# A two-block layer on one core: half of the query weights kept in place of two gather slots, expert products in quadrants

## The reference, cut to what matters

```python
beta = jax.nn.sigmoid(b.astype(f32))
g = -jnp.exp(A_log.astype(f32)) * jax.nn.softplus(a.astype(f32) + dt_bias.astype(f32))
```

```python
mod = (c_act @ w_ada[l] + b_ada[l])[:, None, :]
h = rms_norm(x, g_mix[l]) * (1.0 + scale1) + shift1
proj = h @ w_in[l]
q_a, lat, k_r, iq, ik, iw, q_b, k_b, v_b, f_b = jnp.split(proj, split_at, axis=-1)
o_a = dsa_attention(...)          # over keys that an index picks
o_b = forgetting_attention(...)   # f_b: 8 columns, one forget logit per head
mixed = jnp.concatenate([rms_norm(o_a, g_out_a[l]), rms_norm(o_b, g_out_b[l])], axis=-1)
x = x + gate1 * (mixed @ w_out[l])
h2 = rms_norm(x, g_ffn[l]) * (1.0 + scale2) + shift2
x = x + gate2 * peer_ffn(h2, w_peer_q[l], peer_keys1[l], peer_keys2[l], peer_u[l], peer_v[l])
```

```python
act = jax.nn.gelu(jnp.einsum('cd,chkd->chk', hc, u[expert]), approximate=False)
wgt = (g * act).astype(hc.dtype)
return jnp.einsum('chk,chkd->cd', wgt, v[expert])
```

## Time and profile before

| | us |
|---|---|
| three timed runs | 1416.09, 1419.27, 1419.91 |
| their median | 1419.27 |
| the profiled execution | 1415.75 |
| its span in the trace | 1413.8 |
| TensorE busy | 1301.3 (92%) |
| VectorE, ScalarE, GpSimd busy | 833.5, 275.1, 429.4 |
| DMA | 431.46 MB, mean 305 GB/s |
| granted TensorE clock, mean | 0.989 |

### The profile page before, as it was taken

The page is one execution under the profiler, slowest core; times in us unless marked ns, Lnnn a source line. Parts: engine busy times, 40 slices in busy tenths (PEclk is TensorE's granted clock), DMA queues, the critical chain, the costliest instruction groups (busy, mean ns, idle before and its releaser), DMA issues.

```text
span 1413.8 us, 15154 instructions
## 1 busy us (share of the span) xinstructions
PE 1301.3 (92%) x5447; PEld 837.9 (59%) x5447; DVE 833.5 (59%) x2027; ACT 275.1 (19%) x671; POOL 429.4 (30%) x554
## 2 busy tenths in 40 slices
PE   7999999999999999999999989889998777778776
PEld 6888888888687777757576634445642222222222
DVE  3553466203138888733476777757667667766654
ACT  2013100130010000033332235432220112111101
POOL 0101030000100000000034545555566555655551
PEclk9999999999999999999999999999999999999999
DMA  8345665224469888477369999999999999999995
GB/s 291 121 160 190 228 141 179 75 106 150 134 238 327 289 314 290 178 269 281 141 266 424 422 424 421 421 396 408 425 426 425 425 426 425 426 425 426 425 426 242
DMA packets 120250, 431.46 MB, mean 305 GB/s; under 512 B 10998, under 2 KB 35004, under 8 KB 84592
## 3 DMA queue, kind: packets, MB, share of 16 engines
q0 software_dynamic: 37904, 275.99, 47.6%
q1 hardware_dynamic: 82272, 154.50, 30.4%
HBM read 429.23 MB, written 1.24 MB: 304 GB/s over the span
## 4 chain that ended last, share of the span: by engine, by line
PE 57%; DMA 30%; ACT 4%; DVE 3%; issue 2%; POOL 2%; SPq 1%; POOLq 0%; DVEq 0%; ACTq 0%
PE psum L592 30%; DMA wr<-peer_uv,arena 18%; DMA arena<-peer_uv,arena 7%; PE psum L1140 6%; PE psum L906 4%; PE psum L882 2%; DMA xc<-peer_uv,arena 2%; DMA first_slot<-peer_uv,arena 2%; PE psum L1158 1%; PE psum L957 1%; DVE wr L2419 1%; PE psum L992 1%; POOL arena L2594 1%; PE psum L657 1%; PE psum L1202 1%
## 5 line engine op out<-in xcount | busy, mean ns | idle before, releaser
L592 PE MATMUL psum<-hT,wr 128*128 128x256 f32 x1728 | 377.5, 380 | 0.0
L592 PEld LDWEIGHTS psum<-hT,wr 128*128 128x128 f32 x1728 | 327.0, 190 | 48.1 <-issue 4.0
L1140 PE MATMUL psum<-wr,arena 128*128 128x512 f32 x576 | 277.5, 612 | 38.6 <-POOL arena L2594 38.5
L2419 DVE CUSTOM_DVE_ANT_0 wr<-psum,wr 128x1024 f32<-128x1024 f32 x144 | 176.0, 1222 | 105.7 <-DMA wr<-peer_uv,arena 105.4
L1140 PEld LDWEIGHTS psum<-wr,arena 128*128 128x128 f32 x576 | 102.3, 192 | 179.5 <-issue 178.4
L2594 POOL TENSOR_SCALAR arena<-cst,arena 128x128 f32<-128x128 f32 x256 | 122.7, 479 | 200.9 <-ACT arena L1569 189.4
L2622 POOL DMA_INDIRECT wr<-peer_uv,arena x144 | 143.8, 999 | 64.8 <-PE psum L1140 39.1
L1140 PE MATMUL psum<-arena 128*128 128x512 f32 x256 | 126.6, 619 | 32.7 <-POOL arena L2594 32.7
L1569 ACT ACTIVATE arena<-arena 128x1 f32<-128x1 f32 x256 | 50.8, 202 | 492.6 <-DVE arena L2419 492.2
L2419 DVE CUSTOM_DVE_ANT_0 arena<-psum,arena 128x1024 f32<-128x1024 f32 x64 | 78.3, 1224 | 55.4 <-DMA arena<-peer_uv,arena 55.4
L1140 PEld LDWEIGHTS psum<-arena 128*128 128x128 f32 x256 | 44.5, 192 | 109.9 <-issue 109.7
(11 more groups left out here) (354 smaller groups left out, 1449.4 us busy)
## 6 DMA issues: line engine op xcount, KB each, us to landing
wr<-in_w_in SPq DMA_DIRECT2D x21, 2048.0 KB, 9.0
arena<-in_w_ada SPq DMA_DIRECT2D x12, 2048.0 KB, 10.3
wr<-in_w_up SPq DMA_DIRECT2D x22, 1024.0 KB, 8.1
arena<-piece SPq DMA_DIRECT2D x16, 1024.0 KB, 9.3
wr<-in_w_down SPq DMA_DIRECT2D x5, 2048.0 KB, 9.6
wr<-in_w_a_out SPq DMA_DIRECT2D x2, 2048.0 KB, 8.0
wr<-in_w_b_out SPq DMA_DIRECT2D x2, 2048.0 KB, 8.0
wr<-in_w_o SPq DMA_DIRECT2D x2, 2048.0 KB, 8.1
```

What stands on the lines that cost most here:

```text
L592: mm = nc.tensor.matmul(bank[p % 4][:, f * S:(f + 1) * S], slot(i)[:, k, n * P:(n + 1) * P], act[:, k, :], start=k == 0, stop=k == KT - 1)
L1140: mm = nc.tensor.matmul(bank[(6, 0)[t] + half][:, :], diag[:, n % DIAGS, :], gring[slot_of][:, D + half * BANK:D + (half + 1) * BANK], sta ...
L2419: V.tensor_tensor_reduce(gring[slot_of][:, 0:D], h2[t], gring[slot_of][:, 0:D], 1.0, 0.0, ALU.mult, ALU.add, dots[:, t, c:c + 1]).then_inc ...
```

## The change

It does the following.

- The second half of the query weights stays in its `wr` buffer until tile 1 has used it; its two pieces are no longer read. The two slots that lay there join at set 118. The ring has 5 slots, 6 from the sixth set on, 9 from set 88, 13 from set 118 (before 7, 8, 11, 13). The diagonals are laid one ahead of the gather, not two.
- The expert product of a set is made in quadrants: four products of 64x64 diagonal blocks with 512 columns, in the order low/low, high/high, low/high, high/low (rows of the array, then output partitions), so that bank i holds the positions of half i and its partitions the column halves. `add_experts` puts them together with twice the products on 64 partitions.
- The gates' product is made as two sums of four terms for a and b each, in four groups of 8 output partitions (0, 32, 64, 96); VectorE adds the two sums.
- The forget weights are columns 440 to 447 of tok; `forget(t)` then is a transpose of those columns of `tokp`. The names fb0 and fb1 move later in TensorE's order, and their steps on VectorE and ScalarE with them.
- For tile 1, ScalarE makes `branch_stats(1, 1)` after the last attention step, not in step 6; it empties mb1 at tick 78, not 79, ahead of `branch_stats(1, 0)`; VectorE makes `branch_norm(1, 1)` at tick 76 and `branch_norm(1, 0)` at 81 (before 80). TensorE waits for `orow_done` ahead of the output projection.

```diff
-SLOTS, DIAGS, LAG, LEAD = 7, 8, 2, 2
+SLOTS, DIAGS, LAG, LEAD = 5, 8, 2, 1
...
+TOK = 440 + H
...
-JOIN = {SLOTS: 1, 88: 3, 118: 2}
+JOIN = {SLOTS: 1, 88: 3, 118: 4}
...
-    until("tok", w2[:, :, 512:952], 440, "pair_ready", PAIR["tok0"][0] + 1)
+    until("tok", w2[:, :, 512:952], TOK, "pair_ready", PAIR["tok0"][0] + 1)
...
+PIECES = len(PIECE_FROM) - 2
...
-        gring = [wr[(wpq0 + i // 2 - 1) % NS][:, (i % 2) * 2 * D:(i % 2 + 1) * 2 * D] for i in range(SLOTS - 1)]
-        gring = [first_slot[:, :]] + gring
-        gring += [xc[:, 0:2 * D]] + [region(kb0, 2 * D) for kb0 in (8, 19, 70, 50, 58)]
+        halves_of = [wr[(wpq0 + i // 2 - 1) % NS][:, (i % 2) * 2 * D:(i % 2 + 1) * 2 * D] for i in range(2 * NS)]
+        gring = [first_slot[:, :]] + halves_of[:SLOTS - 1] + [xc[:, 0:2 * D]]
+        gring += [region(kb0, 2 * D) for kb0 in (8, 19, 70, 50, 58)] + halves_of[SLOTS - 1:]
...
-            for k in range(KT):
-                mm = nc.tensor.matmul(bank[4][0:32 + H, 0:S], ab[:, k, :], hT[:, k, :], start=k == 0, stop=k == KT - 1)
+            for k in range(KT // 2):
+                for g in range(2):
+                    for half in range(2):
+                        o = 64 * g + 32 * half
+                        mm = nc.tensor.matmul(bank[4][o:o + H, 0:S], ab[:, half * KT // 2 + k, 32 * g:32 * g + H], hT[:, half * KT // 2 + k, :],
+                                              start=k == 0, stop=k == KT // 2 - 1)
...
+                emptied(pe, ("tok0", "tok1b")[t])
                 o = claim_bank(f"fb{t}")
-                pe.wait_ge(s["small_in"], 48)
-                for k in range(KT):
-                    mm = nc.tensor.matmul(o[0:H, 0:P], fbw[:, k, :], hT[:, k, tiles_of[t]], start=k == 0, stop=k == KT - 1)
-                mm.then_inc(s["pair_ready"], 1)
+                nc.tensor.matmul(o[0:H, 0:P], tokp[:, 440:TOK], ident, start=True, stop=True).then_inc(s["pair_ready"], 1)
...
-                if t == 0:
+                if t == 0 or j >= 2:
                     weights(at["wpq"] + j // 2)
                     w = slot(at["wpq"] + j // 2)[:, :, (j % 2) * 2 * P:(j % 2 + 1) * 2 * P]
...
-                    for half in range(2):
-                        mm = nc.tensor.matmul(bank[(6, 0)[t] + half][:, :], diag[:, n % DIAGS, :],
-                                              gring[slot_of][:, D + half * BANK:D + (half + 1) * BANK], start=c == 0, stop=c == P - 1)
-                        if n == SETS - 1 and half == 0:
-                            mm.then_inc(s["half_done"], 1)
+                    for i, cols in ((0, 0), (1, 1), (0, 1), (1, 0)):
+                        own = quarters[i]
+                        mm = nc.tensor.matmul(bank[(6, 0)[t] + i][quarters[cols], :], diag[own, n % DIAGS, own],
+                                              gring[slot_of][own, D + cols * BANK:D + (cols + 1) * BANK], start=c == 0, stop=c == P - 1)
                     mm.then_inc(s["pe_used"], 1)
...
                 if q == 0:
+                    pe.wait_ge(s["orow_done"], 2)
                     emptied(pe, "mb1")
...
             latent_stats(0)
+            copy_q(0, 0)
             forget(0)
-            copy_q(0, 0)
             copy_index(0)
...
-                if step == 6:
-                    branch_stats(1, 1)
-            until(att_tick(UNITS + 1) + 3)
+            branch_stats(1, 1)
+            until(T_TURN + 1)
+            turn_evac("mb1", 1, lambda k: vcol("g_out_b_2", k))
+            until(T_TURN + 2)
             branch_stats(1, 0)
-            until(T_TURN + 2)
-            turn_evac("mb1", 1, lambda k: vcol("g_out_b_2", k))
...
+            chain(V.tensor_copy(small[:, 5, :], bank[4][64:64 + H, 0:S]))
+            chain.wait()
+            chain(V.tensor_tensor(small[:, 0, :], small[:, 0, :], bank[4][32:32 + H, 0:S], ALU.add))
+            chain(V.tensor_tensor(small[:, 5, :], small[:, 5, :], bank[4][96:96 + H, 0:S], ALU.add))
...
+            def add_experts(t, first):
+
+                for n in range(2):
+                    c = slice(n * BANK, (n + 1) * BANK)
+                    for i, own in enumerate(quarters):
+                        chain(V.tensor_tensor(gated[own, n, :], bank[first + i][quarters[n], :], modb[quarters[n], 3, c], ALU.mult))
+                    chain.wait()
+                    V.tensor_tensor(x[:, t, c], x[:, t, c], gated[:, n, :], ALU.add).then_inc(s["x_final"], 1)
...
-            until(att_tick(UNITS - 1) + 3)
+            until(att_tick(UNITS) + 6)
             branch_norm(1, 1)
             until(att_tick(UNITS + 1) + 2)
             branch_rows(1, 0)
-            until(att_tick(UNITS + 1) + 5)
+            until(T_TURN + 4)
             branch_norm(1, 0)
-            until(T_TURN + 2)
             gain_evac(1)
...
-            dve.wait_ge(s["half_done"], 1)
-            for n in range(2):
-                c = slice(n * BANK, (n + 1) * BANK)
-                if n:
-                    dve.wait_ge(s["pe_used"], SETS)
-                chain(V.tensor_tensor(gated[:, n, :], bank[n][:, :], modb[:, 3, c], ALU.mult))
-                chain.wait()
-                V.tensor_tensor(x[:, 1, c], x[:, 1, c], gated[:, n, :], ALU.add).then_inc(s["x_final"], 1)
+            dve.wait_ge(s["pe_used"], SETS)
+            add_experts(1, 0)
...
-                elif n == 5:
-                    pool.wait_ge(s["pair_ready"], filled("pq03"))
```

More of the change, by code:

```diff
@@ L285, in piece_places @@
     out, turns, before = [], [0, 0, 0], [None, None, None]
-    for j in range(len(PIECE_FROM)):
+    for j in range(PIECES):
         b = j % 3 if j < PIECE_WIDE else j % 2
@@ L445, in program @@
         first_in = [sem(f"first_in{j}") for j in range(KT // 2)]
-        landed = [16 * sum(2 if b[0] in ("up", "ab") else 1 for b in blocks[i % NS or NS:i + 1:NS]) for i in range(len(blocks))]
+        landed = [16 * sum(2 if b[0] in ("up", "ab", "tok") else 1 for b in blocks[i % NS or NS:i + 1:NS]) for i in range(len(blocks))]
         def slot(i):
@@ L520, in _ @@
                         sp.dma_start(ab[:, :, 32 * g:32 * g + H], src[:, :, g * H:(g + 1) * H]).then_inc(w_in[i % NS], 16)
+                elif name == "tok":
+                    sp.dma_start(slot(i)[:, :, 0:440], src).then_inc(w_in[i % NS], 16)
+                    fb = A["w_in_2"][0].rearrange("(k p) n -> p k n", p=P)[:, :, 2488:2488 + H]
+                    sp.dma_start(slot(i)[:, :, 440:TOK], fb).then_inc(w_in[i % NS], 16)
                 elif name == "up":
@@ L976, in token_half @@
                 for k in range(KT):
-                    mm = nc.tensor.matmul(o[:, 0:220], hT[:, k, tiles_of[1]], w[:, k, :], start=k == 0, stop=k == KT - 1)
+                    mm = nc.tensor.matmul(o[:, 0:(220, TOK - 220)[half]], hT[:, k, tiles_of[1]], w[:, k, :], start=k == 0, stop=k == KT - 1)
                 mm.then_inc(s["pair_ready"], 1)
@@ L1163, in _ @@
             emptied(pe, "h0b")
-            by_token(0, "tok", 220)
-            forget(0)
+            by_token(0, "tok", TOK // 2)
             pe.wait_ge(s["ffg_in"], 48)
@@ L1169, in _ @@
             by_feature(0, "qb", 0)
+            forget(0)
             index_rows(0)
@@ L1255, in _ @@
             until(6)
+            forget(1)
             index_rows(1)
@@ L1645, in _ @@
             until(3)
-            copy_bank("tok1b", tokp[:, 220:440], 220)
+            copy_bank("tok1b", tokp[:, 220:TOK], TOK - 220)
             until(6)
-            forget(1)
             copy_q(1, 0)
@@ L1651, in _ @@
             copy_index(1)
+            until(10)
+            forget(1)
             until(11)
@@ L2465, in _ @@
                 route(0, step)
-            forget_logits(1)
             until(4)
             rotate_tok(1)
-            until(10)
+            until(8)
+            forget_logits(1)
+            until(12)
             forget_sums(1)
```

32 lines of the change are left out of this document (17 added, 15 removed), and 4 rows, old and new, of the table names.

## The result

The changed kernel takes 1422.13 us (median of 20 runs, 1418.08 to 1426.07), the kernel before 1417.83 us (20 runs, 1414.68 to 1419.91). The ratio is 1.0030, 95% interval 1.0023 to 1.0037: 4.3 us slower. The forecast was 1412. The profiled execution took 1420.46 us (span 1418.6) against 1415.75 (1413.8).

What follows compares the result with a forecast made beforehand. Bound by TensorE's chain up to 720 us, then by DMA bandwidth. From the profiled 1415.75 us, -4.9 - 1.6 - 0.8 - 1.3 + 1.4 = -7.2 gives 1408.6; with 3.5 carried for the median, 1412 us, range 1404 to 1421 (8 in 10).

Steps and rivals of the forecast that it cites:

- lags: Time from a gathered set's landing (its dot product starts) to the end of its matmuls; undisturbed 4.4 us.
- the forecast's own rule: Gather ring: with S slots a set may lag (S-1) x 2.5 - 3.2 - 0.3 us before the stream runs dry.
- Pieces: Saturated gather stream: two pieces, 2.10 MB, no longer read at 425 GB/s, -4.9 us.
- Six slots: Gather ring until set 88, eight slots before: allowed lag falls from 14.0 to 9.0 us, no cost in the sum.
- dips: Bandwidth drops to 393 and 388 GB/s between 920 and 960 us, 3.2 us lost; half returns, -1.6 us.
- Quadrants: Expert matmuls: four quadrants at once, 1.0 us per set instead of 1.72; off the path, worth something as lag.
- Order and LEAD: Late attention stage: ScalarE's root moved, about 2.5 us less lag near 905 us; diagonals one ahead instead of two, nothing.
- Gates: Chain before the first gather: gate product in four column groups, -0.8 us, bounds -1.6 and +0.9.
- Forget: Chain before the first gather: forget projection inside tok, ScalarE's work covered by qb0b, -1.3 us, bounds -1.5 and 0.
- End: Last set, 255: two extra VectorE operations, +1.4 us, bounds +0.6 and +2.3.
- ring rival: Gather ring: six slots too few if quadrants overlap only in pairs; about 1418 us (1415 to 1421), chance 0.22.
- clock rival: Attention stage: TensorE's gaps keep it at 1.2 GHz, backlog passes 9.0 us of lag; 1432 us, chance 0.11.

Runs made afterwards that it cites:

- C: Part of the change: the quadrants with their ends; its price is 2.0 us with eight slots, 1.6 us with six.
- D: Part of the change: kept weights with six slots, one diagonal ahead and what belongs to them; its price is 3.3 us with full products, 2.8 us with quadrants.
- A: Gates in four column groups; alone on the kernel before: 1417.29 us, ratio 0.9993.
- B: Forget projection moved inside tok; alone on the kernel before: 1417.20 us, ratio 0.9998.
- quadrants undone: Changed kernel with full 128x128x512 products and the old ends of both tiles, all else kept: 1419.11 us, ratio 1.0019 against the kernel before.
- both undone: Changed kernel with full products, eight slots, diagonals two ahead and all 16 pieces read again: 1417.10 us, ratio 0.9996 against the kernel before.

## Why the prediction was wrong

**Where it failed: the lags of the attention stage, and six slots at no price.** The forecast gave the two slots no cost of their own, since every lag was to stay within about 9.0 us. It took 8.8 us at 844.92 for the lag of that stretch, "mostly TensorE backlog", and let it fall to 6; the runs show 10.0 (quadrants) and 10.2 (full products), and six slots cost 6.0 us of stream. The step failed in two ways. First, three sets in slot xc stood for all. The trace has TensorE's signal at the end of each set; by it five sets whose dots begin between 840 and 860 us lag 9.3 to 9.6 us, and the set just ahead of the forecast's row is one of them. Timeline of the kernel before, set 38:

```profile
842.33 1.22 DVE L2419 CUSTOM_DVE_ANT_0 wr<-psum,wr 128x1024 f32<-128x1024 f32 x1
...
849.63 1.98 PE L1140 MATMUL psum<-wr,arena 128*128 128x512 f32 x4
```

851.61 - 842.33 = 9.3 us, over the 9.0 allowed by the forecast's own rule. The longest lag of that trace is not 14.8 but 15.7 us (set 85, dot at 963.23, end at 978.9). And the wait of 5.23 us at 951.91 is for set 76, which lagged 13.2 us, less than the 14.0 allowed: the rule was too kind there already.

Second, the lag was not TensorE's backlog of products alone, which shorter products would clear: in TensorE's fixed order attention pieces stand ahead of the sets, and they take their time and wait for other engines. With full products and six slots (timeline of TensorE, then of GpSimd):

```profile
836.67 1.88 PE L1150 MATMUL psum<-wr,arena 128*128 128x512 f32 x4
841.48 1.09 PE L1085 MATMUL psum<-cst,arena 128*128 128x128 f32 x4 [2.93 <-DVE amax L2214]
842.37 3.11 PE L1150 MATMUL psum<-wr,arena 128*128 128x512 f32 x4
```

```profile
838.83 1.00 POOL L2635 DMA_INDIRECT wr<-peer_uv,arena  x1 [1.49 <-PE psum L1150]
839.87 0.45 POOL L2609 TENSOR_SCALAR arena<-cst,arena 128x128 f32<-128x128 f32 x1
845.75 0.99 POOL L2635 DMA_INDIRECT wr<-peer_uv,arena  x1 [5.43 <-PE psum L1150]
```

TensorE idles 2.93 us for the softmax maximum; the set whose dot began at 835.26 ends at 845.5 (lag 10.2), and the next gather leaves after a wait of 5.43 us. In the changed kernel the same place, with quadrants:

```profile
831.40 1.99 PE L1151 MATMUL psum<-wr,arena 64*64 64x512 f32 x8 [2.23 <-POOL arena L2612]
833.31 1.22 PE L1070 MATMUL psum<-arena 64*128 64x256 f32 x2
...
837.90 1.11 PE L1036 MATMUL psum<-cst,arena 128*128 128x128 f32 x4
838.95 1.99 PE L1151 MATMUL psum<-wr,arena 64*64 64x512 f32 x8
...
841.24 1.00 POOL L2638 DMA_INDIRECT wr<-peer_uv,arena  x1 [5.37 <-PE psum L1151]
...
843.15 1.22 DVE L2443 CUSTOM_DVE_ANT_0 wr<-psum,wr 128x1024 f32<-128x1024 f32 x1
...
846.99 1.23 DVE L2443 CUSTOM_DVE_ANT_0 wr<-psum,wr 128x1024 f32<-128x1024 f32 x1 [1.16 <-DMA wr<-peer_uv,arena]
```

The set of the dot at 830.93 ends at 840.9, lag 10.0; the gather issued at 841.24 has its dot at 846.99, 5.7 us later, as the empty queue of the earlier trace rows, and 3.8 us after the dot before it instead of 2.5. That is the stall, and the forecast had named its sign: dots over 2.5 us apart while GpSimd waited for TensorE. The same bandwidth is lost, but the lag is made of other things here: a late diagonal (2.23 us), then five attention products and two sets without a pause at half clock (the granted clock is 0.50 from 825 to 840 us, and a product as at 833.31 takes 0.70 us in the kernel before). So the half clock has a share in this lag, and what shorter sets alone would have done the runs don't show.

The other stall is at the end of the stage. The forecast counted lags of 8.6 and 10.5 us for sets 78 and 79 and trusted piece wout2 to fill the hole; they are 9.9 and 12.1, and up to 13.1 us for set 83 (with full products and six slots 17.2, so here the quadrants shortened the lag). Timeline of the changed kernel, TensorE and GpSimd:

```profile
956.89 1.12 PE L959 MATMUL psum<-cst,xc 128*128 128x128 f32 x4 [3.78 <-DVE xc L2239]
957.94 1.99 PE L1151 MATMUL psum<-first_slot,arena 64*64 64x512 f32 x8
...
960.23 1.00 POOL L2638 DMA_INDIRECT first_slot<-peer_uv,arena  x1 [4.28 <-PE psum L1151]
```

TensorE waits 3.78 us for the branch's normalised rows, and set 78 and its gather stand behind that wait.

**Step by step.** *Pieces* -4.9: -4.8 of stream, right. *Six slots* had no cost in the sum, and the forecast let 1.6 us of dips return: they cost 6.0 us of stream. All else that lies in the stream gave 0.8 (681.96 to 681.15 without C and D), and the traces with A or B alone, whose dips stay (394 and 397 GB/s at 940 us), have 681.26 and 681.32: filling the dips gave the stream nothing that can be seen. In the variant without C and D 740 to 1000 us run at 422 instead of 417 GB/s, worth 3 us of bytes, yet its last dot comes at the same time. What stands against it is in the traces: each gather's landing is told by sixteen signals. For the last gather of the kernel before the fifteenth comes at 1399.10 and the sixteenth at 1402.30, where the dot begins; in the variant at 1396.73 and 1402.27. Windows of the kernel before, then of the variant:

```profile
1395.00:1400.00 5.00, 4.00 (x9) 1.42 (x9) 2.57 (x5) 0.41 (x2) 0.90 (x2) 1.00 0.45 188
1395.00:1400.00 5.00, 3.98 (x9) 1.37 (x9) 2.60 (x5) 0.41 (x2) 0.90 (x2) 1.00 0.13 52
```

So fifteen of sixteen shares of the transfer gained from the filled dips and the slowest did not, and the dots wait for the slowest. Mean GB/s does not show this. Why one share is slower no run shows. *Quadrants*: a set's eight instructions take 1.09 us at full clock, right; at half clock 1.99. *Order and LEAD*: the forecast gave one ahead nothing. It is no gain, but with six slots the loss without it is 11 us, and without the new order 6.2 us. That order did what the forecast asked of it at 905 us: the lags there are 7.2 us at most, where 8 had been forecast. *Gates* -0.8: -1.15 at the transposes (timeline, answering), -1.0 in the times.

```profile
95.13 1.91 PE L698 MATMUL psum<-hT,wr 128*8 128x256 f32 x32
...
110.95 0.73 DVE L1831 TENSOR_TENSOR_SCAN small<-cst,small 8x128 f32<-8x128 f32 x2
...
111.73 0.41 PE L706 MATMUL psum<-cst,small 8*128 8x8 f32 x4 [0.67 <-DVE small L1831]
```

*Forget* -1.3: nothing. The forecast looked for ScalarE's cover (qb0b) and forgot to ask what the removed products themselves covered: the landing of qb. *End* +1.4: +2.5, 0.2 over its upper bound (+0.6 to +2.3): two more products as said, and the last set at half clock, 1.98 us instead of 1.09. *The head's baseline*: the sum stood on an execution whose head had no stretch at 1.2 GHz in 634 to 680 us; the other traces lose 1.5 us or more there. The forecast carried 3.5 us for the difference to the median, so this is a miss in the head's row, not in the time. Of 20 runs the difference is 2.1 us (1417.83 against 1415.75): with it the same sum would have said 1410.7, and the miss would have been 11.4 us instead of 10.1. The 1.3 us between were luck.

Added up for the trace: the stream is -4.8 (bytes) + 6.0 (slots) + 1.0 (quadrants) - 0.8 (all else) = +1.4, and 1413.8 + 0.9 (head) + 1.4 (stream) + 2.5 (tail) = 1418.6.

**The rivals.** The ring rival was right in kind: 6.3 us over the sum, found 7.9 in the stream, and 1422.1 us against its 1418 (1415 to 1421). But it hung on quadrants that overlap in pairs, which is not so; six slots were too few with full products and with quadrants at the clock that they got. The clock rival saw the clock (0.67 at 1100 us with TensorE busy for 12.9 us of 20, where 16.5 of 20 had 1.00) but not its price: C with its clock costs 1.0 us of stream with six slots (683.40 against 682.36), little more than traces differ anyway, and with eight none (681.09 against 681.15). From 1050 us on the sets take 2.0 us of 2.5, as the forecast said. For certain it is paid once, at the last set; that it lengthens the lags at 840 us is in the rows above, its price there is not separated. The chance of the forecast, 0.62, was too high for a sum whose largest gain stood against an untested allowance.

## What to carry to other kernels

How deep a ring must be is read from the lags of all sets in the trace, not of one slot's, and from what they are made of: here in part from waits of the in-order engine for a third one, which no shorter product mends. Before crediting the removal of work on a chain, look at what was loading under it. A saved byte is only worth its time if the buffer it costs does not stall the stream: one slot given up for half of the bytes did no harm that could be measured, two did. And a higher mean bandwidth is no gain as long as the slowest share of each transfer comes no earlier.

## What the runs showed of the hardware

- Four products on 64x64 quadrants run side by side: eight instructions of 64x64x512 took 1.09 us at full clock, 1.98 to 1.99 at half.
- With quadrants the granted clock fell to 1.2 GHz in many stretches: mean 0.880 to 0.885 in the three profiles of kernels with quadrants, 0.983 to 0.992 in those of kernels with full products.
- In a chain of short attention products (634 to 680 us) the traces have none, one or two stretches of a few microseconds at 1.2 GHz, which cost 1.5 to 2.6 us each. The spans of one kernel differ by 5.7 us in 29 runs (1412.8 to 1418.5), so a single profiled execution tells little of such sizes.
- The dot product of a gather that GpSimd issues into an almost empty queue starts 5.7 us later, in both kernels (720.36 to 726.11, 841.24 to 846.99).
- Of the sixteen signals that tell a gather's landing the last came 2.6 to 5.5 us after the fifteenth at the end of four traces (2.6 changed kernel, 3.0 quadrants undone, 3.2 before, 5.5 both undone), and the dot began with it.
